# Turning the second norm's rows tile by tile: tile 1 behind the outputs, tiles 2 to 4 within tile 1's queries

## What is computed

```
h  = rmsnorm(x) * (1 + scale1) + shift1            # token mixing
proj = h @ w_in                                    # queries, keys, hyena inputs, gates
merged = g_a * (attention @ w_oa) + g_b * (hyena @ w_ob)
x  = x + gate1 * (merged @ w_out)                  # "the outputs"
h2 = rmsnorm(x) * (1 + scale2) + shift2            # "the second norm"
q  = h2 @ peer_wq                                  # 8 heads x 2 halves of 128
s  = q . sub_keys                                  # 128 scores for each of 16 half heads
idx, g = the best 16 of the sums of the best 16 of each half, softmaxed
x  = x + gate2 * sum_k gelu(h2 . u[idx_k]) * g_k * v[idx_k]   # 128 experts a token
```

## Time and profile before

| | |
|---|---|
| Runs | 4857.2, 4844.02, 4852.47 us; median 4852.47 |
| The profiled execution | 4840.91 us, of which the span of the core's work is 4839.1 |
| TensorE busy | 3810.1 us (79%), mean granted clock 0.916 of full speed |
| VectorE busy | 3264.3 us (67%) |
| ScalarE, GpSimd busy | 1555.7 us (32%), 1803.4 us (37%) |
| DMA | 1604.72 MB, mean 332 GB/s; the gathers' queue carries 1395.87 MB |

### The profile page before, as it was taken

One profiled execution on the slowest core, in us unless ns is written; L12 is line 12 of the kernel. 1 busy time (PEld: TensorE's weight loads), 2 busy tenths in 40 slices (PEclk: granted clock), 3 DMA queues, 4 the chain that ended last, 5 costly groups with the idle time before them and its releaser, 6 DMA issues.

```text
span 4839.1 us, 42233 instructions
## 1 busy us (share of the span) xinstructions
PE 3810.1 (79%) x12642; PEld 2041.6 (42%) x12642; DVE 3264.3 (67%) x7651; ACT 1555.7 (32%) x4562; POOL 1803.4 (37%) x1515
## 2 busy tenths in 40 slices
PE   7887889796798666767877679889599777777776
PEld 4546464446453233324533346446455332332222
DVE  2323788768778976666567778877877866755555
ACT  2311241001334434433333323100234444444444
POOL 2330132243334434454444323234233444444443
PEclk8988899998899888988988889999799989999999
DMA  7665377676899989999999767767699999999998
GB/s 272 210 221 199 141 284 285 256 296 229 325 367 408 388 339 403 417 412 378 392 417 421 274 236 281 292 217 279 250 355 359 413 398 414 416 413 421 422 421 345
DMA packets 231552, 1604.72 MB, mean 332 GB/s; under 512 B 27590, under 2 KB 29938, under 8 KB 42908
## 3 DMA queue, kind: packets, MB, share of 16 engines
q0 software_dynamic: 198016, 1395.87, 72.7%
q1 hardware_dynamic: 33308, 206.16, 11.0%
HBM read 1590.62 MB, written 11.30 MB: 331 GB/s over the span
## 4 chain that ended last, share of the span: by engine, by line
PE 36%; DMA 29%; DVE 23%; issue 5%; ACT 5%; POOL 2%; SPq 0%; ACTq 0%; DVEq 0%; POOLq 0%
DMA sb_arena<-in_peer_uv,sb_idx 14%; PE ps L1148 14%; DMA sb_gbufs<-in_peer_uv,sb_idx 12%; PE ps L1044 6%; DVE sb_gbufs L1963 5%; PE ps L1085 4%; DVE sb_arena L1963 3%; DVE sb_eacc L1986 3%; PE ps L725 2%; PE ps L752 2%; DVE sb_arena L1949 1%; ACT sb_small L1418 1%; DVE sb_arena L1951 1%; POOL sb_gbufs L2206 1%; DVE sb_arena L1946 1%
## 5 line engine op out<-in xcount | busy, mean ns | idle before, releaser
L2206 POOL DMA_INDIRECT sb_gbufs<-in_peer_uv,sb_idx x768 | 987.0, 1285 | 1770.8 <-PE ps L1148 746.5
L1148 PE MATMUL ps<-sb_gbufs,sb_dge 128*128 128x512 f32 x1856 | 908.1, 639 | 278.0 <-ACT sb_dge L1438 273.6
L1148 PE MATMUL ps<-sb_arena,sb_dge 128*128 128x512 f32 x1856 | 909.6, 640 | 270.2 <-ACT sb_dge L1438 270.2
L2206 POOL DMA_INDIRECT sb_arena<-in_peer_uv,sb_idx x512 | 614.9, 1201 | 794.4 <-PE ps L1148 694.0
L1963 DVE CUSTOM_DVE_ANT_0 sb_gbufs<-sb_gbufs,sb_keep 128x1024 f32<-128x1024 f32 x512 | 625.3, 1235 | 359.6 <-DMA sb_gbufs<-in_peer_uv,sb_idx 357.6
L1963 DVE CUSTOM_DVE_ANT_0 sb_arena<-sb_arena,sb_keep 128x1024 f32<-128x1024 f32 x512 | 622.2, 1229 | 330.6 <-DMA sb_arena<-in_peer_uv,sb_idx 328.9
L1148 PEld LDWEIGHTS ps<-sb_gbufs,sb_dge 128*128 128x128 f32 x1856 | 362.6, 204 | 788.1 <-issue 388.8
L1148 PEld LDWEIGHTS ps<-sb_arena,sb_dge 128*128 128x128 f32 x1856 | 363.7, 204 | 783.2 <-issue 394.2
L1415 ACT ACTIVATE sb_small<-sb_small 128x2 f32<-128x2 f32 x512 | 104.1, 203 | 1522.6 <-DVE sb_small L1963 1517.4
L1986 DVE SCALAR_TENSOR_TENSOR sb_eacc<-sb_gbufs,sb_small,sb_eacc 128x1024 f32<-128x1024 f32 x299 | 392.0, 1311 | 8.2 <-DVE sb_small L1996 0.8
L1963 DVE CUSTOM_DVE_ANT_0 sb_gbufs<-sb_gbufs,sb_h2p 128x1024 f32<-128x1024 f32 x256 | 317.4, 1259 | 60.2 <-DMA sb_gbufs<-in_peer_uv,sb_idx 60.0
(11 more groups left out here) (273 smaller groups left out, 4315.0 us busy)
## 6 DMA issues: line engine op xcount, KB each, us to landing
sb_ring<-in_w_wq SPq DMA_DIRECT2D x48, 1024.0 KB, 7.2
sb_keep<-in_w_ada POOLq DMA_DIRECT2D x52, 512.0 KB, 6.2
sb_ring<-in_w_hy SPq DMA_DIRECT2D x24, 1024.0 KB, 8.3
sb_ring<-in_w_oab SPq DMA_DIRECT2D x18, 1024.0 KB, 7.2
sb_ring<-in_w_ga SPq DMA_DIRECT2D x16, 1024.0 KB, 8.4
sb_ring<-in_w_gb SPq DMA_DIRECT2D x16, 1024.0 KB, 8.1
sb_ring<-in_w_out SPq DMA_DIRECT2D x14, 1024.0 KB, 5.9
sb_gbufs<-in_peer_uv,sb_idx POOLq DMA_INDIRECT x768, 10.2
```

Source lines behind the costliest of these rows:

```text
L1148: q = pe.matmul(ps[:, c, :], dge[:, b, :], gbuf[b][:, D + c * 512:D + c * 512 + 512], start=(h == 0 and i == 0), stop=(h == HALVES - 1 and ...
L2206: nc.gpsimd.indirect_dma_start(out=gbuf[b], out_offset=None, in_=I["peer_uv"], in_offset=bass.IndirectOffsetOnAxis(ap=idx[:, col:col + 1], ...
```

## The change

The turn becomes two points for the latent tokens. Turn 0, behind the outputs, waits for tile 1's norm alone, transposes its 8 blocks into 2 fills (4 blocks in a bank) and has ScalarE make 2 copies of 128x512 into `hT`. Then come queries 0 to 5 of tile 1; turn 1 follows, waits for all norms, and transposes the 24 blocks of tiles 2 to 4 in 8 fills of 3 with 8 copies of 128x384; then queries 6 to 15 and the last scores. For the prompt the turning is the same as before (8 fills of one block). The first query of each part waits for the copies of its own turn. The latent group has 139 D points.

The turn's estimated length goes from 20 to 4 and the second turn has 4, so `spread()` places the E units anew. `phases()` keeps G, R1 and the V points where they stood among the queries, and turn 1 goes in with query 5 (`["D"] * 5` for `["D"] * 4`).

```diff
+def tail_points(g):
+    first = [("query", 0, i) for i in range(NHP + 1)]
+    out = [("out", q // 4, q % 4) for q in range(4 * g.nt)] + [("turn", 0, 0)]
+    if not g.latent:
+        return out + first
+    return out + first[0:6] + [("turn", 1, 0)] + first[6:] + [("query", 1, i) for i in range(NHP + 1)]
+def turnings(g, p):
+    j0, j1 = g.parts[p]
+    blocks, w = [(c, j) for c in range(KD) for j in range(j0, j1)], 4 if j1 - j0 == 1 and g.latent else j1 - j0
+    return [blocks[k:k + w] for k in range(0, len(blocks), w)]
+def turned_before(g, p):
+    return sum(len(turnings(g, k)) for k in range(p))
...
-        return at + ([20, 6, 8] + [21 * k + 2] * 5 if self.latent else [21 * k + 2] * 8) + [3.5] * (4 * nt) + [20] + ([4.0] * 17 + [7.0] * 17 if self.latent else [7.5 * k + 1] * 17)
+        return at + ([20, 6, 8] + [21 * k + 2] * 5 if self.latent else [21 * k + 2] * 8) + \
+            [{"out": 3.5, "turn": 4 if self.latent else 20, "query": 7.5 * k + 1 if not self.latent else (4.0, 7.0, 0, 0)[w[1]]}[w[0]] for w in tail_points(self)]
...
-        wq = len(pace) - 2 * (NHP + 1)
+        wq = len(pace) - 2 * (NHP + 1) - 1
...
-        order += ["G"] + ["D"] * 4 + ["V", "R1"] + ["D"] * 4 + ["V", "V", "R1"] + ["D"] * 4 + ["V", "V", "R1", "D"]
+        order += ["G"] + ["D"] * 5 + ["V", "R1"] + ["D"] * 4 + ["V", "V", "R1"] + ["D"] * 4 + ["V", "V", "R1", "D"]
...
+                def turn(p):
+                    pe.wait_ge(*at("h2", g.parts[p][1]))
+                    for n, blocks in enumerate(turnings(g, p)):
+                        b = g.lo(n)
+                        claim(b, *at("hT2", turned_before(g, p) + n + 1))
+                        for k, (c, j) in enumerate(blocks):
+                            m = pe.transpose(ps[:, b, k * 128:k * 128 + 128], h2_of(g, j)[:, c * 128:c * 128 + 128], ident[:, :])
+                        m.then_inc(s["tr2"], 1)
+                for what, p, i in tail_points(g)[4 * nt:]:
+                    if what == "turn":
+                        turn(p)
+                    else:
...
+                        if i == 0:
+                            pe.wait_ge(*at("hT2", turned_before(g, p + 1)))
...
+                def turned(p):
+                    for n, blocks in enumerate(turnings(g, p)):
+                        act.wait_ge(*at("tr2", turned_before(g, p) + n + 1))
+                        (c0, j0), (c1, j1) = blocks[0], blocks[-1]
+                        act.activation(v.hT[:, c0:c1 + 1, j0 * 128:j1 * 128 + 128],
+                                       ps[:, g.lo(n), 0:len(blocks) * 128].rearrange("p (c t) -> p c t", c=c1 + 1 - c0), ACT.Copy).then_inc(s["hT2"], 1)
```

More of the change, by code:

```diff
@@ L127, in totals @@
             ea_ps=2 * EARLY * self.latent, th=16 - 2 * EARLY * self.latent, mm=8, mg=8, dgr=4, row_ps=8, row=8, out_ps=4 * nt, r2=4 * nt, xadd=4 * nt,
-            ss2=nt, h2=nt, tr2=8, hT2=8, **{n: NHP * len(self.parts) for n in ("qh_ps", "qh", "sc_ps", "sc")}, ctx=32 if self.latent else 0,
+            ss2=nt, h2=nt, tr2=turned_before(self, len(self.parts)), hT2=turned_before(self, len(self.parts)), **{n: NHP * len(self.parts) for n in ("qh_ps", "qh", "sc_ps", "sc")}, ctx=32 if self.latent else 0,
             state=0 if self.latent else 32)
@@ L1064, in dense @@
                     yield
-                pe.wait_ge(*at("h2", nt))
-                for c in range(KD):
-                    claim(g.lo(c), *at("hT2", c + 1))
-                    for j in range(nt):
-                        m = pe.transpose(ps[:, g.lo(c), j * 128:j * 128 + 128], h2_of(g, j)[:, c * 128:c * 128 + 128], ident[:, :])
-                    m.then_inc(s["tr2"], 1)
-                yield
-                pe.wait_ge(*at("hT2", KD))
-                for p, (j0, j1) in enumerate(g.parts):
-                    kind, w0, w1 = ("wq", "wr")[p], j0 * 128, j1 * 128
-                    for i in range(NHP + 1):
+                def turn(p):
[10 more added lines that the diff above has]
+                    else:
+                        j0, j1 = g.parts[p]
+                        kind, w0, w1 = ("wq", "wr")[p], j0 * 128, j1 * 128
                         n = NHP * p + i
+                        if i == 0:
+                            pe.wait_ge(*at("hT2", turned_before(g, p + 1)))
                         if i < NHP:
@@ L1097, in dense @@
                             m.then_inc(s["sc_ps"], 1)
-                        yield
+                    yield
             def spectra():
@@ L1353, in dense @@
                     yield
-                for c in range(KD):
-                    act.wait_ge(*at("tr2", c + 1))
-                    act.activation(v.hT[:, c, 0:T], ps[:, g.lo(c), 0:T], ACT.Copy).then_inc(s["hT2"], 1)
-                yield
-                for p, (j0, j1) in enumerate(g.parts):
-                    w = (j1 - j0) * 128
-                    for i in range(NHP + 1):
-                        n = NHP * p + i
+                def turned(p):
[4 more added lines that the diff above has]
+                                       ps[:, g.lo(n), 0:len(blocks) * 128].rearrange("p (c t) -> p c t", c=c1 + 1 - c0), ACT.Copy).then_inc(s["hT2"], 1)
+                for what, p, i in tail_points(g)[4 * nt:]:
+                    if what == "turn":
+                        turned(p)
+                    else:
+                        w, n = (g.parts[p][1] - g.parts[p][0]) * 128, NHP * p + i
                         if i < NHP:
@@ L1846, in best_sixteen @@
                     link(m)
-                for p in range(len(g.parts)):
-                    for i in range(NHP + 1):
+                for what, p, i in tail_points(g)[4 * nt + 1:]:
+                    if what == "query":
                         if i >= 1:
@@ L2143, in dense @@
                     yield
-                for _ in range(1 + (NHP + 1) * len(g.parts)):
+                for _ in tail_points(g)[4 * nt:]:
                     yield
```

## The result

| | before | after |
|---|---|---|
| Median of 20 runs each | 4844.17 us (4830.62 to 4857.2) | 4860.49 us (4843.65 to 4878.92) |
| Ratio | | 1.0026, 95% interval 1.0016 to 1.0035 |
| Profiled execution, span | 4840.91, 4839.1 us | 4860.62, 4858.8 us |
| Mean granted clock | 0.916 | 0.913 |

A forecast was written before the change was run, and what follows sets the result against it. No engine owned the chain of waits; VectorE's list ended last ahead of the first latent gather. Gap gains of 16.4 us less 8.6 for moved units gave 7.8, from the median 4852.5 to 4844.7 us, range 4832 to 4858.

The forecast's parts named there:

- What the moved units cost where they land: Ahead of the merges, in attention and convolutions: 3 units at VectorE's 1.43 us, 4.3 us a layer, 8.6 in all.
- the gap: From outputs to first latent gather: VectorE's shorter list starts the routing earlier, gaining 7.5 us in layer 1, 8.9 in layer 0.
- the upper bound: In attention and convolutions: the moved units cost at most 9.9 us a layer, a pair's share of a gather's round trip.
- The clock: Tile 1's first queries in layer 1: slow after 15 us idle, 3.6 us for query 0 and 2.4 for query 1.
- Turn 1: Behind the first routing: costs nothing, its work taking 8.3 us of the 9.9 before VectorE asks for the score.
- No carry: Rival: earlier latent gathers wait in their buffers, so only the 8.6 us of cost remain: 4861 us, chance 0.05.
- Units free: Rival: moved units cost nothing in attention and convolutions, so the whole 16.4 us stay: 4836.1 us, chance 0.27.
- The gather round trip paces them: Rival: at points 12 to 68 one pair more a layer costs 9.9 us, 19.8 against 16.4: 4855.9 us, chance 0.18.

The follow-up runs named there:

- e9: The changed kernel with its E units from point 44 to 78 four ahead of the order before: 4846.96 us, ratio 0.9999 to before.
- e11: The kernel before with two E units a layer moved forward from points 62 and 64 to 44 and 46: 4849.69 us, ratio 1.0002.
- e10: The changed kernel with before's E unit order up to point 61 and the four more units behind point 62: 4851.49 us, ratio 1.0008 to before.
- e4: The kernel before with four E units a layer moved from the turning to points 12, 16, 20 and 24: 4862.06 us, ratio 1.0024.
- e5: e3 with four more E units a layer moved out of the attention into the merges: 4834.55 us, ratio 0.9968 to before.
- e3: The changed kernel with before's E units up to the merges, the six or seven freed from the gap put into the merges: 4832.63 us, ratio 0.9969 to before.

## Why the prediction was wrong

**What failed is one term: "What the moved units cost where they land".** The prediction put it at 3 units of 1.43 us, 4.3 a layer and 8.6 in all. The stretch up to the last output product grew by 14.0 and 14.8, 28.8 in all. The prediction named this as what would make it wrong ("more than 8 us a layer"). In layer 1, 1.4 of that is the unit among the outputs, which the prediction had set against the gap's gain (in layer 0 that unit stands behind the last product), so the like of the 8.6 is about 27. Even the upper bound, 9.9 a layer from the gather's round trip, was too low, and the sum came out with the other sign: -18.3 + 28.8 and not -16.4 + 8.6.

Two things were missed, and the runs tell their sizes at the first merge, both layers together, where after is later by 25.6 us:

- **The place: 12.8 us.** This is after less e9 (25.6 - 12.8). The times agree: e9 is at 0.9999 and after at 1.0026, 13 us apart, with intervals that don't meet. The step table shows where it arises, and layer 0's share of it is in part the clock behind TensorE's wait. Not all of it is lost in every case: e11's layer 1 gave it back, and e11 as a whole is no slower than before. The prediction counted the units ahead of each stretch but never asked which of the four stands at each of its points. That could be read from the trace of before: the short convolution falls between two additions, and ScalarE's copies end 0.9 us ahead of TensorE's need.
- **A pair of units in its number: 12.8 us with e9, 17.9 with e10, 20.5 with e4**, so 4.3 to 11.2 a layer, 8.5 in the mean of the six, with the scatter of single profiles in them. In time e4 costs 11.6 us for both layers (0.24%), after some of it came back in the gap. The upper bound, 9.9, was about right for this half of the cost alone. VectorE's own 1.43 us a unit (5.7 a pair) was the lower end and not the value. VectorE busy for 88% was read as "VectorE's time is the price". Why it is more isn't shown by a run of its own; the rows of after have more waits of each engine for another, gathers among them.

Why a pair costs some 10 us a layer when added (e4) and gives at most 4 ahead of the merges when taken away (e5 beside e3) stays open, and so do the 3.5 to 3.8 us of the attention.

**The gap was forecast rightly.** First gather behind the last product: 34 and 30 us forecast, 34.3 and 30.0 measured. From the end of the last product to the routing, layer 0: 22.6 forecast, 22.5 measured (1179.68 to 1202.13, and 31.5 in the earlier trace rows); layer 1: 18.4 forecast (3406.7 to 3425.1), 18.2 measured (3433.87 to 3452.04), 27.3 in the earlier trace rows. In its steps: product's end to the last copy 4.2 and 4.3, from there to the routing 14.2 and 13.9. The 7.5 of layer 1 was this gain of 8.9 less the 1.4 of the added output unit, which the table of the two traces counts ahead of the product.

**The clock.** Queries 0 and 1 took 5.74 us (forecast 6.0), 1.9 more than in the earlier trace rows, and 6.57 in layer 0. The windows over the two, in after (granted clock is the first number behind the busy columns):

```profile
3438.20:3443.90 5.70, 5.69 (x34) 5.70 (x34) 4.23 (x13) 0.28 (x1) 0.00 (x0) 0.65 0.00 0
3444.00:3452.00 8.00, 8.00 (x74) 8.00 (x73) 6.36 (x32) 1.10 (x4) 0.00 (x0) 1.00 0.72 260
```

A mean of 0.65 of full speed, between the 1.2 and the 2.4 GHz level, after 19.8 us of waiting, and full speed from the third query on. The rule that the prediction cited from the Trainium skill (TensorE: Matmul & The Clock Gate, "HAM oscillation — how this bites in real kernels") agrees with these rows. Its price in the gap was small beside the term that failed. Where it had no place in the prediction, behind the new wait in layer 0's transform, it was 2.6 us.

**Turn 1** cost nothing, as forecast: from the exponential (3455.21) to query 5's score behind it (3461.05) 5.8 us, where 8.3 were allowed, and VectorE didn't wait. In layer 0 the score was there at 1211.2 and VectorE took it up at 1213.2.

**No carry** is out: from first gather to the next mark 1542.8 and 1544.0, 1395.0 and 1395.3.

**The rivals.** "Units free" is out. "The gather round trip paces them" had the right sign and nearly the time (3.4 above before; the ratio says 7.8 to 17.0), at 0.18 too small a chance, and its mechanism is only part: with the data halved, 19.5 of 23 us stay by the medians, 16 of 26 by the ratios. None of the rivals held a place in the cycle.

## What to carry to other kernels

- When filler work of a fixed cycle is spread over a list that all engines follow in order, moving it changes two things: how much lies ahead of a point, and which member of the cycle meets it. Count modulo the cycle at the points where the engines wait for each other, and move whole cycles where you can.
- Where two engines are both busy for 85% or more, don't take one engine's duration as the price of an added unit. Here a pair with 5.7 us of VectorE's time cost 4.3 to 11.2 us a layer, 8.5 in the mean, near the 9.9 of the gathers' round trip.
- Put what a gap gives up where one engine is alone in being busy (here the merges, e3: 15 us), and write that placement down; a change to a length that steers a spreading rule moves every unit.

## What the runs showed of the hardware

VectorE and GpSimd held each other up where both had operands in SBUF. Timeline of after, layer 0's last outputs:

```profile
1177.54 0.72 POOL L2174 TENSOR_TENSOR sb_x<-sb_x,sb_arena 128x256 f32<-128x256 f32 x1 [6.76 <-DVE sb_arena L1846]
1177.57 1.78 DVE L2018 SCALAR_TENSOR_TENSOR sb_eacc<-sb_gbufs,sb_small,sb_eacc 128x1024 f32<-128x1024 f32 x1
...
1179.60 1.27 DVE L2018 SCALAR_TENSOR_TENSOR sb_eacc<-sb_gbufs,sb_small,sb_eacc 128x1024 f32<-128x1024 f32 x1
1179.76 1.69 POOL L2174 TENSOR_TENSOR sb_x<-sb_x,sb_arena 128x256 f32<-128x256 f32 x1 [1.50 <-DVE sb_arena L1846]
```

Whichever began first took 0.72 and 1.27 us, and the other took longer, 1.78 for 1.27 and 1.69 for 0.72: by 0.5 and 1.0 us, about what the first still had to run (0.7 and 1.1). The Trainium skill (SBUF — State Buffer, "SBUF: two separate sides") says that the pair of ports which the two share is locked for a whole instruction, also for a VectorE operation with two inputs in SBUF against a GpSimd operation that reads SBUF; these rows agree. The issue of a gather on GpSimd varies too, between 0.94 and 1.98 us in the attention and the convolutions of layer 1. That this is the same lock is an inference from what runs beside it. In after the first issue of a pair stands beside the second of two additions; in before the first stands beside the convolution (an input in PSUM), and the second beside an addition and a product:

```profile
3042.61 1.87 POOL L2238 DMA_INDIRECT sb_gbufs<-in_peer_uv,sb_idx  x1 [8.21 <-DVE sb_eacc L2018]
3044.78 0.95 POOL L2238 DMA_INDIRECT sb_gbufs<-in_peer_uv,sb_idx  x1 [0.31 <-issue]
```

```profile
3028.23 0.94 POOL L2206 DMA_INDIRECT sb_gbufs<-in_peer_uv,sb_idx  x1 [7.42 <-DVE sb_eacc L1986]
3030.87 1.69 POOL L2206 DMA_INDIRECT sb_gbufs<-in_peer_uv,sb_idx  x1 [1.70 <-DVE sb_eacc L1986]
```

Here the first gather of the pair is issued in 1.87 us and not in 0.94, and the second in 0.95 and not in 1.69. No run took this effect alone, so its share in the step is not known.
